# Handing mixer steps to the dense work by kind of stage instead of evenly, in a two-layer encoder trunk on one core

## The reference

```
h = RMSNorm(x);  proj = h @ W_in
x = x + concat(AxialGQA(8 heads), BiGLA(4 heads), BiMLSTM(4 heads)) @ W_out
[g | u] = depthwise conv of width 3 (RMSNorm(x) @ W_up)
x = x + (silu(g) * u) @ W_down          # 2816 wide
```

## Time and profile before

| | |
|---|---|
| median of 3 runs | 3155.12 us (3153.72 to 3170.22) |
| the profiled execution's own time | 3158.78 us |
| its span | 3157.0 us |
| mean granted clock of TensorE | 0.956 |

### The profile page before, as it was taken

How to read it: one execution, slowest core, us unless ns; L and a number is a source line. 1 busy time by engine, 2 the same in 40 slices (tenths; PEclk the granted TensorE clock), 3 DMA queues, 4 the chain that set the end, 5 groups by cost and what they waited for, 6 DMA issues and landing times. The chain is left out here.

```text
span 3157.0 us, 40532 instructions
## 1 busy us (share of the span) xinstructions
PE 2884.0 (91%) x16272; PEld 2360.8 (75%) x16272; DVE 1888.6 (60%) x3051; ACT 1342.6 (43%) x2131; POOL 0.2 (0%) x4
## 2 busy tenths in 40 slices
PE   5988879789899999989899999999989998999998
PEld 5967768678677778978676677887867777777787
DVE  4743755455666666655566767564656576566665
ACT  3331545345434554246533444325563354343332
POOL 0000000000000000000000000000000000000000
PEclk9987889889999999999999999999989999999999
DMA  3311101101121112211121111231111121232222
GB/s 121 111 40 42 41 27 34 54 34 61 62 73 67 67 67 100 105 67 55 46 74 67 61 67 67 74 111 54 54 61 67 61 73 55 80 107 87 100 94 80
DMA packets 64231, 218.55 MB, mean 69 GB/s; under 512 B 7342, under 2 KB 9006, under 8 KB 64046
## 3 DMA queue, kind: packets, MB, share of 16 engines
q1 hardware_dynamic: 64046, 215.98, 19.2%
HBM read 211.76 MB, written 4.19 MB: 68 GB/s over the span
## 5 line engine op out<-in xcount | busy, mean ns | idle before, releaser
L498 PE MATMUL ps<-hh,wlo 128*128 128x512 f32 x1696 | 694.0, 409 | 20.3 <-DVE hl L1403 11.1
L500 PE MATMUL ps<-hh,whi 128*128 128x512 f32 x1696 | 675.8, 398 | 0.0
L499 PE MATMUL ps<-hl,whi 128*128 128x512 f32 x1696 | 675.0, 398 | 0.0
L1355 DVE TENSOR_TENSOR wlo<-raw,whi 128x1024 fp32r<-128x1024 f32 x388 | 472.8, 1219 | 87.6 <-ACT whi L947 86.8
L947 ACT ACTIVATE whi<-raw 128x1024 fp32r<-128x1024 f32 x388 | 404.2, 1051 | 104.4 <-DMA raw<-d_w_units 104.0
L498 PEld LDWEIGHTS ps<-hh,wlo 128*128 128x128 f32 x1696 | 324.4, 191 | 99.3 <-issue 18.2
L500 PEld LDWEIGHTS ps<-hh,whi 128*128 128x128 f32 x1696 | 323.9, 191 | 73.3
L499 PEld LDWEIGHTS ps<-hl,whi 128*128 128x128 f32 x1696 | 324.5, 191 | 66.0
L498 PE MATMUL ps<-acth,wlo 128*128 128x512 f32 x704 | 301.8, 429 | 57.7 <-DVE x L1543 44.7
L1543 DVE TENSOR_TENSOR x<-x,ps 128x512 f32<-128x512 f32 x352 | 239.8, 683 | 160.2 <-PE ps L500 157.7
L499 PE MATMUL ps<-actl,whi 128*128 128x512 f32 x704 | 286.5, 407 | 0.0
(11 more groups left out here) (264 smaller groups left out, 4055.5 us busy)
## 6 DMA issues: line engine op xcount, KB each, us to landing
raw<-d_w_ffn SPq DMA_DIRECT2D x264, 512.0 KB, 3.2
raw<-d_w_units SPq DMA_DIRECT2D x124, 512.0 KB, 3.3
x<-d_x_in SPq DMA_DIRECT2D x24, 256.0 KB, 6.5
d_x_out<-x SPq DMA_DIRECT2D x16, 256.0 KB, 3.1
ropec<-d_rope SPq DMA_DIRECT2D x3, 128.0 KB, 4.1
ropes<-d_rope SPq DMA_DIRECT2D x3, 128.0 KB, 3.9
cmask<-d_chunkmask SPq DMA_DIRECT2D x1, 256.0 KB
w2s<-d_w2p SPq DMA_DIRECT2D x1, 256.0 KB
```

Source lines behind the costliest of these rows:

```text
L498: pe.matmul(out, stat[1], mov[0], start=first, stop=False)
L499: pe.matmul(out, stat[0], mov[1], start=False, stop=False)
L500: return pe.matmul(out, stat[0], mov[0], start=False, stop=last)
L1355: dve.tensor_tensor(wlo[:, SLOT[u], :, :], raw[:, SLOT[u], :].rearrange("p (k c) -> p k c", k=KT), whi[:, SLOT[u], :, :].bitcast(F32), ALU ...
```

## The change

`weave` takes a list of shares, one for each mixer step, and hands out step i after the first dense slot k with share * over < k + 1. The list comes from `pace(n)`: each step has a weight, the share of step i is the sum of the weights ahead of it over the sum of all. Nothing is added to or taken from the work of any engine; the order of the instructions in the lists of PE, ACT and DVE changes. The special lead of 10 steps in the prelude goes.

```diff
-M_STEPS = 149
-M_OVER = 276
-PRELUDE, LEAD = 2, 5
+PRELUDE = 2
+
+ATT_PACE = ((5, 4.0), (34, 1.0))
+GLA_PACE = ((5, 4.0),) + ((9, 3.0), (16, 1.7)) * 2 + ((4, 2.0),)
+LSTM_PACE = ((10, 2.0), (32, 2.0), (4, 3.0))
+MIX_PACE = ((5, 2.0),)
+
+def pace(n):
+    stages = (GLA_PACE, LSTM_PACE, ATT_PACE, MIX_PACE) if n == 0 else (ATT_PACE, GLA_PACE, LSTM_PACE, MIX_PACE)
+    weights = [w for stage in stages for count, w in stage for _ in range(count)]
+    return [sum(weights[:i]) / sum(weights) for i in range(len(weights))]
...
-def weave(dense, slots, mixer, over, lead=()):
+def weave(dense, slots, mixer, shares, over):
     done = 0
     for k in range(slots):
         next(dense)
-        if k < len(lead):
-            until = sum(lead[:k + 1])
-        else:
-            until = sum(lead) + (k + 1 - len(lead)) * (M_STEPS - sum(lead)) // (over - len(lead))
-        while mixer is not None and done < min(M_STEPS, until):
+        while done < len(shares) and shares[done] * over < k + 1:
             next(mixer)
             done += 1
...
-            weave(in_projection(1), P_STEPS, mixers(0), P_STEPS - 4)
+            weave(in_projection(1), P_STEPS, mixers(0), pace(0), P_STEPS - 4)
...
-            weave(ffn(0), PRELUDE + F_SLOTS, mixers(1), M_OVER, (LEAD,) * PRELUDE)
+            weave(ffn(0), PRELUDE + F_SLOTS, mixers(1), pace(1), F_SLOTS - 12)
...
-                weave(ffn(n - 1), F_SLOTS, mixers(n), M_OVER)
+                weave(ffn(n - 1), F_SLOTS, mixers(n), pace(n), F_SLOTS - 12)
```

More of the change, by code:

```diff
@@ L166, in weave @@
         next(dense)
-        if k < len(lead):
-            until = sum(lead[:k + 1])
-        else:
-            until = sum(lead) + (k + 1 - len(lead)) * (M_STEPS - sum(lead)) // (over - len(lead))
-        while mixer is not None and done < min(M_STEPS, until):
+        while done < len(shares) and shares[done] * over < k + 1:
             next(mixer)
             done += 1
-    while mixer is not None and done < M_STEPS:
+    while done < len(shares):
         next(mixer)
@@ L177, in weave @@
     for gen in (dense, mixer):
-        if gen is not None:
-            assert next(gen, None) is None
+        assert next(gen, None) is None
 def alone(gen):
```

## The result

The kernel after takes 3142.25 us (median of 7, 3132.56 to 3148.95) beside 3155.12 us (median of 7 of the kernel before). The ratio is 0.9945, 95% interval 0.9923 to 0.9967: faster by about half a per cent. The forecast was 3069 us with a range of 3010 to 3137: the sign was right, the size was not. Of the 86 us the medians show 13, and the ratio some 17.

The account below looks back on a forecast made before the run. PE bounds the kernel, losing time in the weaves to waits and the lower clock. Waits won, 62 us, plus 24 us of clock make 86 us off 3158.8, so 3072.8, or 3069 against the median; range 3010 to 3137.

Parts of the forecast that it names:

- Gates and decays beside the FFN: GLA's gate and decay steps in the FFN weaves: more dense work between them wins 16 us plus 22 us.
- The term for the down tiles: GLA's gates and decays beside the FFN: 22 of 36 us of PE's down-tile waits go.
- The term for the key transposes: GLA's decays beside the FFN: more dense work covers PE's waits at the key transposes, winning 16 us.
- First weave, GLA: Key transposes in the first weave: 6 us won at the first, 4 for the second direction, 10 in all.
- First weave, mLSTM and attention: First weave: the opening gains, one more rotation in mLSTM loses; 0 us, from -12 to +10.
- The clock: All weaves: time at the lower clock level shrinks as the waits do; 24 us back, bounds 0 and 50.
- rival (4): Steady attention: fewer long dense matmuls make the clock fall there, 68 us lost, time 3137 us; chance 0.05.
- Openings: Attention's openings: 11 us won at the second weave and prelude, 2 us in the third and fourth weave.
- End of mLSTM: mLSTM's last four steps: 0.94 more slots each cover waits of up to 2.8 us; 5 us won.
- rival (1): Whole kernel: waits only move, as steps stand behind others on DVE's strict list; time 3145 to 3155 us, chance 0.09.
- Steady attention: Steady attention steps get fewer slots and pay 4 us over all weaves, bounds 0 and 40.
- Rival (2): Steady attention becomes the bound as PE waits for ACT's exponential; slower, 3197 us at 1 us a step; chance 0.06.

Follow-up runs that it names:

- GLA flat: Kernel after, but in the FFN weaves all 59 GLA steps have the same weight (same sum): 3168.76 us, ratio 1.0032 to the kernel before.
- The edit of the wait: Kernel after, but PE's second key transposes of a direction wait for the fifth of DVE's eight products instead of the eighth: 3124.53 us, ratio 0.9895.

## Why the prediction was wrong, step by step

**Gates and decays beside the FFN: half right, half a wrong mechanism.** The term for the down tiles (22 of 36 us) held by their row: over the run it fell by 20.7 us; in the third weave it fell from 19.5 to 7.2, and GLA flat brings 6.8 of that back. Two corrections belong to it. The 5.7 us of the second weave, behind `accg`, were an up tile's and not a down tile's; they went too. And down tiles that no longer wait for `add_down` in GLA wait for the low part of their weight instead, some 10 us of the 22.7 above. The term for the key transposes (16 us) is the step that failed first: their waits beside the FFN fell from 17.0 to 14.2 us. I took the wait for the end of a chain that runs over seven steps, and set 31 us of dense work against it. The timeline of DVE and PE in the kernel after shows that the chain lies within one step:

```profile
1578.21 0.68 DVE L1659 TENSOR_TENSOR ktil<-ktil,qkG 128x512 f32<-128x512 f32 x1
1578.82 0.68 DVE L1659 TENSOR_TENSOR qtil<-qtil,qkG 128x512 f32<-128x512 f32 x1
1579.42 0.68 DVE L1659 TENSOR_TENSOR khat<-khat,qkG 128x512 f32<-128x512 f32 x1
1580.02 0.68 DVE L1659 TENSOR_TENSOR qhat<-qhat,qkG 128x512 f32<-128x512 f32 x1
...
1580.76 0.66 PE L809 MATMUL ps<-ident,ktil 128*128 128x128 f32 x4 [1.79 <-DVE qhat L1659]
```

DVE's four products and PE's second transposes are the same step k = 7. PE needs `ktil`, the first, and waits for `qhat`, the fourth. No pace puts dense work inside a step; the releaser in the earlier trace rows, `qhat` and not `ktil`, had said so. The edit of the wait won 17.7 us of medians.

**First weave, GLA (10 us).** The wait at the first key transposes went, more of it than forecast, and came back 10 us long at a dense tile. PE goes on at nearly the same time in both kernels. Timeline of PE in the kernel before, then of ACT and PE in the kernel after:

```profile
200.79 1.12 PE L803 MATMUL ps<-ident,ktil 128*128 128x128 f32 x4 [12.48 <-DVE ktil L1653]
```

```profile
191.06 1.28 ACT L1156 ACT_TABLE_LOAD   x1
192.36 1.15 ACT L1156 ACTIVATE e<-e,ones 128x1024 f32<-128x1024 f32 x1
...
197.99 0.23 ACT L1199 ACTIVATE aL<-G 128x16 f32<-128x16 f32 x1 [2.23 <-DVE G L1633]
...
199.76 0.64 ACT L1000 ACTIVATE tokB<-ps 128x256 f32<-128x256 f32 x2
...
200.27 0.55 PE L504 MATMUL ps<-whi,hl 128*128 128x256 f32 x1 [10.00 <-ACT tokB L1000]
```

I counted dense slots as cover. But dense slot 16 needs a PSUM bank that ACT copies out in the same slot, behind the gates' logarithms and a wait for DVE's scans in ACT's strict list. Dense work that needs the same engine as the chain covers it only as far as that engine's next duty. This is read from the timelines; no run moved that copy.

**First weave, mLSTM and attention (0 us).** `key_query` rises by some 6 us there (12.3 to 18.6): two heads now wait 6.5 us, one of them behind the second rotation that I had named (DVE at 420.0 to 423.6, the head at 428.9). And 12.3 us appear ahead of the row transposes, 2.5 before by the list of waits. I had blamed `head_squares` once I saw it; the run that moved them left 10.3 us. What lengthens this opening stays open. The run with the new pace in the first weave alone shows that this weave's pace as a whole costs 0.4%.

**The clock (24 us back; none came in the profiled pair).** I tied the lower level to waits. In the first weave it stood over two chunk stretches whose rows show PE busy for 41.97 of 42 and 37.95 of 38 us, and the 13 us that this weave lost in the profiled pair are time at the lower level. The new pace had taken dense slots from these very steps (1.06 instead of 1.23); whether that is the reason stays open, since the same order has also run one of them at the full clock. My rival (4) looked for a fall of the clock in steady attention, where it is not (0.99 in the third and fourth weave). The Trainium skill, "TensorE: Matmul & The Clock Gate", Part 1, ties the level to PE's being busy; these rows, busy throughout at 0.59, do not fit that, and the measurement decides, unless the busy time of these rows is not what the level follows, which no run here tells. In the FFN weaves the forecast fared better: 46 to 34 us in the third and fourth. Nor is the profiled execution the usual one: with the middle clock of the seven runs, 0.961, the lower level makes 2 x 0.039 x 3140 = 245 us of the span, and with the middle clock of the kernel before, 0.956 to 0.958 in three sets of 11 to 20 runs, 265 to 278. By that the lower level shrank by 20 to 33 us, an estimated 7 to 11 us of time at the third that I had taken.

**Openings (11 + 2).** The second weave's transposes wait less, but the fill does not: 11.9 us at `hl` over the run, 9.6 of them in the second weave, where I had 2.3. I take the two openings that now stand between the fill's slots on DVE to be the reason; no run shows it. In the third and fourth weave the two uncovered openings were foreseen at 2.5 us each; the second took 5.2. Timelines of ACT, DVE and PE, kernel after:

```profile
1399.47 0.76 ACT L1065 ACTIVATE accv<-ps,cw 128x512 f32<-128x512 f32 x1
1400.13 0.62 ACT L1113 ACTIVATE qd<-tokA 128x512 fp32r<-128x512 f32 x1
...
1401.90 0.69 DVE L1538 TENSOR_TENSOR accv<-accv,accg 128x512 f32<-128x512 f32 x1
1402.51 0.68 DVE L1585 TENSOR_TENSOR qd<-tokA,qd 128x512 fp32r<-128x512 f32 x1
...
1404.28 1.94 PE L707 MATMUL ps<-ident,qd 128*128 128x128 f32 x8 [5.20 <-DVE qs L1595]
```

The split of queries stands behind the FFN's value start on ACT and its convolution and product on DVE; slots without dense PE work are not without ACT and DVE work.

**End of mLSTM (5 us).** The wait ahead of `mix` went (5.4 us), and 10.5 us stand inside `mix`, where 2.4 stood before: moved.

**mLSTM, priced at nothing beside the FFN.** It kept its pitch and changed its neighbours, as rival (1) said, and that cost. ACT and DVE at its first head, kernel after:

```profile
1799.27 1.28 ACT L1059 ACT_TABLE_LOAD   x1
...
1802.51 2.44 ACT L1282 ACTIVATE Dt<-mR,CT 128x128 f32<-128x128 f32 x8
...
1805.66 0.75 DVE L1529 SCALAR_TENSOR_TENSOR accv<-ps,cw,accv 128x511 f32<-128x511 f32 x1 [4.55 <-ACT accv L1065]
...
1807.11 1.67 DVE L1820 SCALAR_TENSOR_TENSOR Dt<-ps,Dt 128x512 f32<-128x512 f32 x4
```

A Silu now falls between the exponentials, a value start behind them, and DVE's `weigh` behind the convolution; PE waits 6.3 us.

**Steady attention (-4 us): right.** Its transposes wait 9.9 us in 25 pieces of at most 0.6, 4.9 of them beside the FFN. Rival (2) falls: one slot between steps nearly covers the chain.

So the sum failed by adding waits won without asking what each waiting tile needs next: 74 us of waits went, against 66 in the sum, and 58 came elsewhere, where the sum had 4. Of rival (1), to which I gave 0.09, this kernel has the larger part: in the third weave the runs with later mLSTM and earlier openings change two places and keep their sum (-4.9 + 4.1, -7.7 + 7.9 us).

## What to carry to other kernels

Before a wait is priced as curable by distance, look whether producer and consumer lie in the same step and whether the consumer waits for more than it reads: one constant here was worth about as much as all the pacing. Cover counts only if the covering work does not itself need the engine that runs the chain, so follow its next buffer to the engine that frees it. After a re-pacing, list what the moved steps now stand behind on every strict list, those at an unchanged pitch too. And read the clock of a stretch from several executions before giving it a cause.

## What the runs showed of the hardware that was not expected

PE ran 42 us at a mean clock of 0.59 with almost no idle time in its rows (41.97 us busy), and 33.5 us at 0.95 over the same steps with a matmul of 128x512 added to each. The same order of instructions without the addition ran the second chunk stretch at 0.72 in one execution and at 1.00 in another, 38.0 and 29.1 us. The same addition at the even pace left one stretch at 0.73 in one run and at 0.68 in another, so it is no sure remedy. Leaving out Silu, and with it 85 table loads of 1.28 us each on an engine that is busy 43% of the span, took 38 us off.
